# Two-block transformer on one core: six of eleven up-projection tiles in seven block products, the modulation sums started earlier, one convolution tap on ScalarE

## The reference

```python
mod = silu(c) @ w_mod[layer] + b_mod[layer]       # 1024 -> 6 * 1024
shift1, scale1, gate1, shift2, scale2, gate2 = split(mod, 6)
h = rmsnorm(x, g_attn[layer]) * (1.0 + scale1) + shift1
o = mixer_layer(h, ...)                           # attention, ends with o @ w_out
x = x + gate1 * o
h = rmsnorm(x, g_mlp[layer]) * (1.0 + scale2) + shift2
up = h @ w_up[layer]                              # 1024 -> 2 * 2816
u, g = up[..., :2816], up[..., 2816:]
g = causal_depthwise_conv(g, conv_w[layer], conv_b[layer])   # width 3
x = x + gate2 * ((silu(g) * u) @ w_down[layer])   # 2816 -> 1024
```

## Time and profile before

| | us |
|---|---|
| median of 3 runs | 1944.18 |
| lowest, highest run | 1943.29, 1944.21 |
| the profiled execution: time / span | 1942.48 / 1940.7 |
| PE busy | 1653.6 (85%) |
| DVE busy | 710.2 (37%) |
| ACT busy | 285.6 (15%) |
| POOL busy | 142.3 (7%) |
| mean granted TensorE clock | 0.937 |

### The profile page before, as it was taken

How to read it: one execution, slowest core, us unless ns; L and a number is a source line. 1 busy time by engine, 2 the same in 40 slices (tenths; PEclk the granted TensorE clock), 3 DMA queues, 4 the chain that set the end, 5 groups by cost and what they waited for, 6 DMA issues and landing times.

```text
span 1940.7 us, 24600 instructions
## 1 busy us (share of the span) xinstructions
PE 1653.6 (85%) x10484; PEld 943.2 (49%) x10484; DVE 710.2 (37%) x1482; ACT 285.6 (15%) x773; POOL 142.3 (7%) x149
## 2 busy tenths in 40 slices
PE   8999999999999999999786766757999785756757
PEld 3456988544579964474432232322474432232322
DVE  1583666977628976274010010101274110010101
ACT  1243000021511001253000010001253000010000
POOL 0011000000214510310000000000220000000000
PEclk9999999999999999999897987979999898987978
DMA  9992788755235643646999999999745999999998
GB/s 354 341 338 73 249 303 299 273 196 184 88 119 185 236 151 126 192 174 259 403 429 431 427 432 426 433 429 407 252 174 238 389 430 431 425 431 427 434 428 349
DMA packets 164164, 599.75 MB, mean 309 GB/s; under 512 B 18928, under 2 KB 78064, under 8 KB 140272
## 3 DMA queue, kind: packets, MB, share of 16 engines
q1 hardware_dynamic: 163838, 598.03, 78.4%
q10 hardware_dynamic: 242, 0.53, 0.1%
HBM read 594.75 MB, written 3.80 MB: 308 GB/s over the span
## 4 chain that ended last, share of the span: by engine, by line
PE 57%; DMA 38%; DVE 3%; ACT 1%; issue 1%; POOL 0%; SPq 0%; DVEq 0%; ACTq 0%
DMA extra<-in_w_down 14%; DMA extra<-in_w_up 12%; DMA extra<-in_w_gate 11%; PE ps L1266 9%; PE ps L1379 6%; PE ps L1332 6%; PE ps L1304 5%; PE ps L1619 5%; PE ps L949 4%; PE ps L1118 4%; PE ps L1517 3%; PE ps L1216 3%; PE ps L1639 1%; DMA ring<-in_w_mod 1%; PE ps L835 1%; PE ps L857 1%
## 5 line engine op out<-in xcount | busy, mean ns | idle before, releaser
L1619 PE MATMUL ps<-ring,wide 128*32 128x256 f32 x2912 | 217.9, 465 | 120.8 <-DMA ring<-in_w_up 76.2
L1619 PEld LDWEIGHTS ps<-ring,wide 128*32 128x32 f32 x2912 | 107.3, 133 | 225.3 <-DMA ring<-in_w_up 85.8
L1639 PE MATMUL ps<-ring,wide 128*32 128x512 f32 x768 | 158.7, 641 | 45.6 <-DMA ring<-in_w_down 41.9
L3204 DVE TENSOR_TENSOR wide<-ps,wide 128x512 f32<-128x512 f32 x16 | 10.7, 670 | 508.1 <-PE ps L1619 508.1
L1266 PE MATMUL ps<-hT,ring 128*128 128x256 f32 (+1 forms) x1088 | 183.8, 330 | 0.0
L1266 PEld LDWEIGHTS ps<-hT,ring 128*128 128x128 f32 x1088 | 166.6, 191 | 17.3 <-issue 2.9
L1619 PE MATMUL ps<-extra,wide 128*32 128x256 f32 x1056 | 89.9, 512 | 62.7 <-DMA extra<-in_w_up 40.3
L1379 PE MATMUL ps<-ring,hT 128*128 128x512 f32 (+2 forms) x320 | 127.3, 555 | 0.4 <-issue 0.4
L1639 PEld LDWEIGHTS ps<-ring,wide 128*32 128x32 f32 x768 | 44.7, 117 | 155.5 <-issue 122.4
L2375 DVE SCALAR_TENSOR_TENSOR extra<-ring,sc,extra 128x512 f32<-128x512 f32 x140 | 109.8, 784 | 5.2
L1619 PEld LDWEIGHTS ps<-extra,wide 128*32 128x32 f32 x1056 | 41.9, 146 | 109.5 <-DMA extra<-in_w_up 44.2
(11 more groups left out here) (372 smaller groups left out, 2102.6 us busy)
## 6 DMA issues: line engine op xcount, KB each, us to landing
ring<-in_w_gate SPq DMA_DIRECT2D x24, 4096.0 KB, 31.4
ring<-in_w_down SPq DMA_DIRECT2D x24, 4096.0 KB, 33.7
ring<-in_w_up SPq DMA_DIRECT2D x20, 4096.0 KB, 32.6
ring<-in_w_mod SPq DMA_DIRECT2D x24, 2048.0 KB, 12.9
ring<-in_w_up SPq DMA_DIRECT2D x44, 1024.0 KB, 8.0
extra<-in_w_gate SPq DMA_DIRECT2D x8, 4096.0 KB, 35.1
extra<-in_w_up SPq DMA_DIRECT2D x8, 4096.0 KB, 33.0
ring<-in_w_in SPq DMA_DIRECT2D x13, 2048.0 KB, 13.0
```

Of the source, the lines that this page charges most:

```text
L1619: last = mm(ps[2 * part + e // 2][j * CAP:(j + 1) * CAP, e % 2 * 2 * P:(e % 2 + 1) * 2 * P], xsT[:, k, e * CAP:(e + 1) * CAP], expert_row( ...
L1639: last = mm(ps[6 + n][e * CAP:(e + 1) * CAP, :], hidT[:, e, k, :], expert_row(n0, e, k)[:, n * N:(n + 1) * N], start=k == 0, stop=k == KD - 1)
```

## The change

Four things change together.

1. `UP_WHOLE` becomes `(5, 2)`: in the first layer tiles 5 to 10 go through `up_seven` too, with all its sums and joins.
2. The first layer's modulations 10 to 21 move: tables (`FOLD_AFTER`, `READ_AFTER`, `SUM_WHOLE`, `SUM_FIRST`, `SUM_PARTS`) say after which step each is summed, folded and read. Numbers 10 and 11 are now summed within the output projection; nine of the twelve are folded before tile 5, 17 and 18 right before it. A third buffer for row sums lies in `wide`. `B1_TILES` follows `FOLD_AFTER`, so the tiles are transferred in the new order.
3. In both layers the convolution's first tap with the bias is a ScalarE activation (`tap`), so `conv` is four VectorE instructions instead of six; within `up_seven` the convolution of tile j-1 now stands ahead of the joins of tile j.
4. In both layers `up_second` of the first seven-product tile stands ahead of `up_rows_sums`; the power for one norm moves behind the sums on GpSimd's list.

The lines of SyncE that name `(0, "up", 4)` and `(0, "up", 8)` are not changed.

```diff
-LAGS = (2, 6)
...
-UP_WHOLE = (11, 2)
-UP_PARTS = {3: (0, range(0, 3)), 4: (0, range(3, 6)), 5: (0, range(6, 8)), 6: (1, range(0, 4)), 7: (1, range(4, 8))}
+UP_WHOLE = (5, 2)
+FOLD_AFTER = ({("out", 1): (10, 11), ("up", 1): (12, 13), ("up", 2): (14, 15), ("up", 3): (16,), ("up", 4): (17, 18),
+               ("up", 7): (19,), ("up", 9): (20,), ("down", 2): (21,)}, {("up", 6): (0,), ("up", 7): (1,)})
+READ_AFTER = ({1: (12, 13), 2: (14, 15), 3: (16,), 8: (19,), 10: (20,)}, {6: (0,), 7: (1,)})
+SUM_WHOLE = {0: (14,), 1: (15,), 2: (16, 17), 3: (18,)}
+SUM_FIRST = ({5: (19, range(0, 2)), 6: (19, range(4, 6)), 7: (20, range(0, 2)), 8: (20, range(4, 6))}, {})
+SUM_PARTS = ({5: (19, range(2, 4)), 6: (19, range(6, 8)), 7: (20, range(2, 4)), 8: (20, range(6, 8))},
...
-        tiles += [(l, "out", j) for j in range(2)]
-        late = MODS[l][EARLY[l]:]
-        steps = [(l, "up", j) for j in range(UPT)] + [(l, "down", j) for j in range(NDOWN)]
-        for n, t in enumerate(steps):
+        tiles.append((l, "out", 0))
+        for t in [(l, "out", 1)] + [(l, "up", j) for j in range(UPT)] + [(l, "down", j) for j in range(NDOWN)]:
             tiles.append(t)
-            if LAGS[l] <= n < len(late) + LAGS[l]:
-                tiles.append((late[n - LAGS[l]][0], "mod", late[n - LAGS[l]][1]))
+            tiles += [(MODS[l][q][0], "mod", MODS[l][q][1]) for q in FOLD_AFTER[l].get(t[1:], ())]
     return tiles
 
...
+def _up_acts(l):
+    first = UP_WHOLE[l]
+    acts = [(what, j) for j in range(first - 1) for what in ("tap", "silu")]
+    for j in range(first, UPT):
+        acts += [("tap", j - 1), ("copy", j), ("silu", j - 1)]
+    return acts + [("tap", UPT - 1), ("silu", UPT - 1)]
+
...
+        def mod_bank(L, q):
+
+            if L or q > FOLD_AFTER[0][("up", UP_WHOLE[0] - 1)][-1]:
+                return MOD_BANK
+            if q >= EARLY[0]:
+                return 4 + 2 * (q % 2)
+            return 4 + q % 2 if q < MOD_AT[LAST_IN][0] else 7 - q % 2
+
+        def mod_sum(L, q):
+
+            if L == 0 and q >= EARLY[0]:
+                return (acc[:, 1, :], wide[:, FCH * T:FCH * T + N], acc[:, 0, :])[q % 3]
+            return acc[:, q % 2, :]
...
+                        if j > first:
+                            pe.wait_ge(*up_read(s, L, m, j - 1))
+                        elif m == 6 and L == 0:
+                            pe.wait_ge(*s.at("b1_mod_ready", FOLD_AFTER[0][("up", first - 1)][-1] + 1))
                         elif m == 5:
-                            pe.wait_ge(*s.at("b1_product_ready", 2))
+                            pe.wait_ge(*s.at("b1_product_ready", first - first % 2))
...
+                def folds(step):
+                    for q in FOLD_AFTER[L].get(step, ()):
+                        modulation(q)
+
+                folds(("out", 1))
                 up(0, P, P)
                 up(1, P, P)
-                late = len(MODS[L]) - EARLY[L]
...
+                def tap(j):
+
+                    y = sm[:, j % 2, :].rearrange("p (f t) -> p f t", f=2)
+                    act.wait_ge(*up_block(s, L, 4, j))
+                    gp = ps[2 * (j % 2) + 1][:, :].rearrange("p (f t) -> p f t", f=2)
+                    if j >= UP_WHOLE[L]:
+                        act.wait_ge(*up_read(s, L, 4, j))
+                        gp = up_joined(j)[:, 1, :, :]
+                    for f in range(2):
+                        av(y[:, f, :], gp[:, f, :], ACT.Identity, scale=cc1(L, "conv_w", 2 * FCH + 2 * j + f),
...
+                for what, j in UP_ACTS[L]:
+                    if what == "tap":
+                        tap(j)
+                    elif what == "silu":
+                        silu(j)
+                    else:
+                        up_copies(j)
...
                 which = 2 * L + 1
                 out_residual(0, 0)
+                if L == 0:
+                    accumulate(10)
                 out_residual(0, 1)
                 norm_stream(which, 0)
                 out_residual(1, 0)
                 evac_stream(which, 0, 24)
+                if L == 0:
+                    accumulate(11)
                 out_residual(1, 1)
                 norm_stream(which, 1)
                 evac_stream(which, 1, 24)
+                if L == 0:
+                    accumulate(12)
+                    mod_out(10)
+                    accumulate(13)
+                    mod_out(11)
 
                 def conv(j):
...
                 def conv(j):
 
-                    dve.wait_ge(tile_done, b1_used(B1_AT[(L, "up", j)]))
-                    if j >= 2:
-                        dve.wait_ge(*silu_done(s, L, j - 2))
+                    dve.wait_ge(*up_act(s, L, "tap", j))
                     y = sm[:, j % 2, :].rearrange("p (f t) -> p f t", f=2)
                     gp = ps[2 * (j % 2) + 1][:, :].rearrange("p (f t) -> p f t", f=2)
                     if j >= UP_WHOLE[L]:
                         gp = up_joined(j)[:, 1, :, :]
-                    dve.wait_ge(*s.own())
-                    for f in range(2):
-                        ts(y[:, f, :], gp[:, f, :], cc1(L, "conv_w", 2 * FCH + 2 * j + f), cc1(L, "conv_b", 2 * j + f),
-                           ALU.mult, ALU.add).then_inc(s.up(), 1)
                     for tap_, sh in ((1, 1), (0, 2)):
-                        dve.wait_ge(*s.own())
+                        if tap_ == 0:
+                            dve.wait_ge(*s.own())
                         for f in range(2):
...
-                for j in range(UPT):
-                    if j < UP_WHOLE[L]:
-                        if L == 0 and j == UPT - 1:
-                            down_sums(0)
-                        if L and j == 1:
-                            up_rows_sums()
-                            up_second(2)
-                        conv(j)
-                        if L == 0 or j == 0:
-                            up_gated(j)
-                        if L == 0 and j == UPT - 1:
-                            down_sums(1)
-                        if L == 0 and j < late:
-                            accumulate(EARLY[L] + j)
-                    else:
-                        up_join(j, UP_READS[:1])
-                        up_fourth(j)
-                        up_gated(j - 1)
-                        if j in UP_PARTS:
-                            accumulate(*UP_PARTS[j])
-                        if j == UPT - 1:
-                            down_sums(0)
-                        up_join(j, UP_READS[1:])
-                        conv(j)
-                        if j == UPT - 1:
-                            up_gated(j)
-                            down_sums(1)
+                    for q in READ_AFTER[L].get(j, ()):
+                        mod_out(q)
+
+                first = UP_WHOLE[L]
+                for j in range(first - 1):
+                    conv(j)
+                    up_gated(j)
+                    if L == 0:
+                        for q in SUM_WHOLE[j]:
+                            accumulate(q)
+                up_second(first)
+                up_rows_sums()
                 if L == 0:
-                    mod_out(EARLY[L] + UPT - LAGS[L])
+                    mod_out(17)
+                    mod_out(18)
+                for j in range(first, UPT):
+                    if j in SUM_FIRST[L]:
+                        accumulate(*SUM_FIRST[L][j])
+                    conv(j - 1)
+                    up_join(j, UP_READS[:1])
+                    up_fourth(j)
+                    up_gated(j - 1)
+                    if j in SUM_PARTS[L]:
+                        accumulate(*SUM_PARTS[L][j])
+                    if j == UPT - 1:
+                        down_sums(0)
+                    up_join(j, UP_READS[1:])
+                conv(UPT - 1)
+                up_gated(UPT - 1)
+                down_sums(1)
                 down_sums(2)
                 down_sums(3)
                 if L == 0:
-                    accumulate(EARLY[L] + UPT)
-                    mod_out(EARLY[L] + UPT + 1 - LAGS[L])
+                    accumulate(21)
                 down_sums(5)
                 down_sums(4)
                 if L == 0:
-                    mod_out(EARLY[L] + UPT + 2 - LAGS[L])
+                    mod_out(21)
                     ab(1, 0, "g_attn")
                     ab(1, 1, "g_mlp")
 
```

148 lines of the change are left out of this document (77 added, 71 removed).

## The result

The changed kernel takes 1970.62 us (median of 4 runs, 1968.65 to 1971.03) against 1944.2 us before (4 runs beside it): ratio 1.0134 [1.0121, 1.0147], slower by 26.4 us. Its profiled execution has a span of 1968.9 us, 28.2 more than before. The forecast was 1966 and the range 1952 to 1972.

A forecast was written before the change was run, and what follows sets the result against it. PE was taken to bound the first block, which is all the change touches. Terms 28.1 + 1.9 + 2.5 - 8.0 - 2.2 = +22.3 on the profiled 1942.48 gave 1964.8, as a median 1966; range 1952 to 1972.

The forecast's parts named there:

- gap ahead of fold 18: First layer, before tile 5: PE waits from 262.4 to 290.5 for VectorE's sum behind the late bias row, 28.1 us.
- wait for up tile 4: First layer: tile 4's weights land at 247.7 behind copies and router weights in a full queue; PE waits 1.9 us.
- slower clock: PE starts slower after a gap, at granted clock 0.50, as in the second block; 2.5 us added.
- six tiles in seven products: First layer: six tiles at 12.51 us instead of 13.84 for a whole tile, 8.0 us gained.
- second layer, first such tile: The second layer's first seven-product tile loses both its waits, for `up_second` and tile 1's product: 2.2 us gained.
- sum over twelve tiles at 5.8 us: First layer's DMA queue from 198.9: latency, twelve tiles, copies with router weights and the row put the row's landing at 283.8.
- signs: Trace near 262: PE gap 25 to 31 us, bias row landing some 20 after issue, DMA share 1.0 from 200 to 282.
- Part 2: First tap on ScalarE, both layers: nothing gained on PE except 2.2 us in the second layer's first seven-product tile.
- Row early: Rival: the bias row gets past the queue, landing at 269.9; PE waits 14.2 us ahead of fold 18; 1952.6; chance 0.10.
- No change: Rival: row in time, copies still fill the queue, PE waits 7.0 us ahead of fold 18; 1943 to 1945; chance 0.03.
- Faster: Rival: neither row nor queue delays the first layer, only the 10.2 us of gains stay; 1934; chance 0.05.
- The queue is worse: Rival: router issue costs 16.09 us, not 10.9, all lands 5.2 later; 1971; chance 0.05 together with seven products spoilt.

The follow-up runs named there:

- row_early: Changed kernel with the `b_mod` bias row issued ahead of up tile 2 instead of up tile 8: 1961.15 us, 1.0086 of the kernel before.
- three moves: Changed kernel with bias row issued earlier, bias copies and router weights behind the first layer, sums 19 and 20 one tile later: 1938.21 us, ratio 0.9966 to kernel before.
- pool_short: Three moves with GpSimd's sums of weight blocks in seven-product tiles cut to part of their columns: 1938.19 us, 0.9963 of the kernel before.
- tap_back_second: Three moves with the convolution's first tap back on VectorE in the second layer's seven-product tiles alone: 1935.76 us, 0.9964 of the kernel before.
- tap_back: Three moves with the convolution's first tap back on VectorE in all seven-product tiles of both layers: 1944.13 us, 1.0006 of the kernel before.
- gap_filled: Changed kernel with 24 matmuls, whose result nothing reads, in PE's gap ahead of fold 18: 1969.26 us, 1.0142 of the kernel before.
- gap_filled_32: Changed kernel with 32 matmuls, whose result nothing reads, ahead of fold 18: 1971.92 us, 1.0148 of the kernel before.

## Why the prediction was right

The direction, the place and the mechanism were right: the wait of `mod_out(16)` for a row of `b_mod` that SyncE issues behind a full queue, with the seven products' gain whole beside it. The size was too small, 22.3 for 28.2 us. That 1970.62 still lies in the range, 1.4 below its upper end, is in part luck: that end stood there for a worse queue, and most of the surplus came from the clock and the tap. By the terms of the sum, from the profiled executions:

| term | predicted | measured |
|---|---|---|
| gap ahead of fold 18 | 28.1 | 24.7 |
| wait for up tile 4 | 1.9 | 3.7 |
| slower clock | 2.5 | 3.7 behind the gap, 2.7 in tile 4 |
| waits in the first layer's down part | 0 | 0.5 (0.27 and 1.98 for 1.70) |
| six tiles in seven products | -8.0 | -8.0 (6 x (13.84 - 12.51)) |
| second layer, first such tile | -2.2 | -2.2 |
| second layer, fold of modulation 1 | 0 | 1.5 |
| rest of the first block; second block | 0 | 0.6; 1.0 |
| sum | 22.3 | 28.2 (terms rounded) |

The 13.84 us of a whole tile were worked out with the fold at 255.48, which isn't in the stretch, in place of the one at 240.81; with that one they are 13.82, and the term stays at 8 us. The first layer's down part waited 1.70 in the kernel before too:

```profile
392.11 1.99 PE L1332 MATMUL ps<-extra 128*128 128x512 f32 x4 [1.70 <-DVE extra L2828]
```

**The gap.** The row landed at 284.97 where I had 283.8, and the sum was ready at 291.6 where I had 290.5. That sum over twelve tiles at 5.8 us was the best number of the prediction. The gap is shorter than 28.1 because PE came 4.5 us later to it (1.8 more wait, 2.7 of slow tile). I had the row issued at 262.9; SyncE was held by the full queue until 272.37. It made no difference, since the data queue and not the issue set the landing. So three of the signs that I had named came out beside their numbers: the gap at 24.7 for 25 to 31, the issue at 272 for 262 with the landing 12.6 us later instead of some 20, and the DMA share at 0.88 from 230 to 245 us in place of 1.0.

**The clock** is the term that was sized wrong: 6.4 for 2.5. I had taken it from one pair of rows with 6.13 idle, 2.5 lost, and had not applied it to the wait for tile 4, which I knew of; behind the long gap 3.7 were lost.

**Part 2 failed in the second layer.** "Both ends give nothing on PE" was argued from VectorE's slack in a window. The window's mean was right and the fold's place was not looked at: conv now waits for ScalarE's tap, VectorE stands idle for 1.22 a tile where before it had 0.74 of its own work to do, and every step that comes after it is later. In the first layer the same sentence failed the other way: there the tap on ScalarE was worth 5.9 us to PE. VectorE's timeline of the changed kernel in the second layer, and the tap in that of the kernel before:

```profile
676.28 0.42 DVE L2874 TENSOR_TENSOR extra<-extra,ps 128x256 f32<-128x256 f32 x1
677.92 1.79 DVE L2826 SCALAR_TENSOR_TENSOR spare<-extra,fixed,spare 128x255 f32<-128x255 f32 x4 [1.22 <-ACT spare L1961]
```
```profile
649.84 0.74 DVE L2750 TENSOR_SCALAR spare<-extra,fixed 128x256 f32<-128x256 f32 x2
```

The three runs without the fold's wait and with whole sums on GpSimd are those with the tap back. And the earlier trace rows gave GpSimd's 12.94 of 25 only as room, not as what slows VectorE's steps.

**The rivals.** "Row early", a small DMA that gets past the queue, didn't happen. "No change" had 7.0 ahead of fold 18 for a row in time behind the copies, and row_early measured 6.59 there, but with 1961 in place of 1943 to 1945: the rival had left out the slow matmuls of tile 4 (3.1) and the wait for the product with the slow matmuls behind it (4.4), and in that execution the second layer's attention took 3.3 more. "Faster" is what the three moves made true, by another order as it said, at 1938 in place of 1934. "The queue is worse", 1971, came nearest the time by another way: the queue was as I counted, and most of the surplus was the clock and the tap. The seven products brought all of their 8 us in the changed kernel already.

The Trainium skill, "DMA: Bandwidth & Descriptors", section "Queues, rings and completion order", which says that completion isn't in issue order within one issuing engine, changed nothing here: by the earlier trace rows and by the changed kernel the row lands 1.3 us behind the tile in front of it.

Open: the first layer gained 6.2 us of the 8.0 with the three moves (start of the up projection to start of the second layer's input projection), of which the waits of 0.66, 0.27 and 0.28 more at the down projection explain 1.2; 0.6 isn't traced. What lengthened a stretch of the second layer's attention in some profiled executions (15.07 us in three_moves and pool_short for matmuls that took 12.06 in tap_back_second, the clock at 0.50 for a while) wasn't tried. By those rows it makes up to 3 us of one execution.

## What to carry to other kernels

When work is moved to an earlier place, ask of every small operand that it needs where its DMA stands in the issue order, and count the queue from there with the data of all that is ahead: bytes over the measured rate gave the landing to 1.2 us. A wait on the bound engine can cost more than its length, so give the clock a term for each wait, also for the short ones: in the up and down projections of these first layers slow matmuls followed each wait of 2.59 us or more, and those of 1.98 us in some executions. And an operation that goes to a slack engine can cost there where its consumer now waits for a handover; look at each layer by itself, as the same move gained 5.9 us in one and lost 1.7 in the other.

## What was unexpected of the hardware

- The granted clock fell to half after waits as short as 2.82 us (row_early, tile 4 in 17.11) and 3.67 (16.80, clock 0.51), where a tile takes 14.06. In gap_filled, where the wait for the same tile was 1.22, it took 14.08 at 1.00.
- In three_moves' second layer the clock was 0.50 from 495 to 500 us behind waits of only 0.25 and 0.69. In tap_back_second the same matmuls had the same two waits, and the clock stayed at 1.00.
- The wait of 1.98 at the down projection, the same to 0.01 in all of them, was followed by four matmuls in 1.98 us with the three moves, in 2.84 in tap_back, 3.13 in pool_short and 3.63 in gap_filled_32. What decides that I haven't found.
- VectorE's instructions with two operands in SBUF took twice their time or more beside GpSimd's sums: 6.03 for 3.13 (sum steps), 3.78 for 1.79 (convolution), 1.75 for 0.68 (product). Only for the sum steps was the cause tested, by cutting GpSimd's sums short; for the others it is read from where they fell.
- SyncE was held 22.38 us for six issues in a full queue, and what it issued next still landed within 1.2 us of where the data ahead of it had put it in the prediction.
